# Attention groups scored one ahead and normalised one behind, with decay rows in bf16, rotation on one engine and a weight split at every side step

## The chip, the cores and the metric

One core of one Trainium2 chip runs the kernel. The metric is the device time of one execution in microseconds (us), lower is better. Engines are called PE (TensorE), DVE (VectorE), ACT (ScalarE), POOL (GpSimd) and SP (SyncE). The difference that a measurement of this kernel can tell from none is about 0.3%.

## What is computed

The reference runs two stacks of two layers on a sequence of 256 tokens with 1024 channels, in float32.

```
first_block, for layer 0 and 1:
    x = x + norm(mixer(norm(x)))       mixer: even_mixer (layer 0) or diff_mixer (layer 1)
    x = x + norm(memory_cross_attention(norm(x), norm(mem)))      4 heads of 64
    x = x + norm(swiglu(norm(x)))
even_mixer: fox attention, 8 heads: softmax(q k^T / 8 + (c_q - c_k)), c = cumsum(log_sigmoid(f)), causal
            nsa attention, 8 heads: compressed, selected and window keys, each gated by a sigmoid
diff_mixer: 8 heads: p = softmax(q1 k1^T / 8) - lam * softmax(q2 k2^T / 8), o = p v
second_block, for layer 0 and 1:
    x = x + 0.5 * swiglu_2(norm(x))
    z = norm(x) @ w_in; neighborhood attention (8 heads, a bias table), gated linear attention,
        latent attention (4 heads, 192 wide), each projected and gated; x = x + mixed @ w_out
    x = x + 0.5 * swiglu_2(norm(x))
partial rotation (rope) of q and k: x1' = x1 c - x2 s, x2' = x2 c + x1 s
```

A fox row's own term c_q cancels in the softmax, so the kernel adds only -c_k to the scores.

## The kernel before

**Weights.** All weight matrices are one stream of units of at most 2048 columns by 128 partitions. `load` (L419 on) brings a unit into one of 6 raw slots over SP's queue. `part` splits it: ACT casts it to fp32r (`w_hi`, L450), DVE subtracts that from the raw value (`w_lo`, L455), into 3 high slots. A product of two fp32 matrices is three fp32r matmuls (`three_products`, L594 to L596). Outside attention a unit is split in one piece, by `prepare`. Inside attention (`turn["gentle"]`) it is split in 4 pieces (PIECES), one at a time by `trickle`. When PE's next matmuls need a unit that isn't whole, `take` puts out all its missing pieces at once.

**Side work.** `fillers` is a list of generators (the input projections' later columns, memory keys and values, compression, gates). Each step of one, a side step, is some 12 matmuls on a quarter of a unit, or a group of transposes with its evictions. `fill(n)` puts out n side steps. Every engine runs its instructions in the order in which the Python puts them out, and waits on semaphores in that order.

**Attention** (`attention`, L777 on) takes groups of two heads: 16 groups in the even mixer (4 fox, then 4 times selected, window and compressed keys), 8 in the diff mixer, 2 in each memory attention, 4 in each neighborhood attention (with `bias`), 2 in each latent attention. A group's parts are:

- `scores`: PE writes two heads' scores into two banks. Mask rows come by bf16 matmuls (L806), q k^T by fp32 matmuls (L812); a fox group has a second fp32 matmul per score block with `ident` rows as weights and `c_neg` (8 partitions) as data.
- `maxed`: DVE takes the row maxima (L843) and scales them (L846); with a bias it first adds the bias (L836) and reduces that (L839).
- `exped`: ACT takes the exponentials into `probs` with their sums (L868).
- `normed`: DVE takes a reciprocal per head (L887), in gated groups a product with the gate (L890), and scales `probs` (L894).
- `turned`: PE transposes `probs` (L909), waiting for `normed`.
- `copied`: ACT (L922) and DVE (L928) copy the transposed weights into `pT`.
- `summed`: PE multiplies them with the values (L953 for the diff mixer, L959, L966). The result is evicted by ACT (L986) and DVE (L991, the low part), in the diff mixer by ACT alone (L977). In the even mixer the selected and window groups of a head pair are not evicted; their sum goes on in the compressed group.

The order of the parts is written out by hand at the end of `attention`:

```
for i in range(len(groups) + 1):
    trickle(2)
    scores(i); turned(i - 1); maxed(i)
    copied(i - 1); exped(i)
    fill(a); normed(i); summed(i - 1); fill(b)
```

The pair (a, b) is (3, 3) for the first groups of the two mixers and (1, 1) for the rest, (5, 5) in the neighborhood attention, (2, 2) in the latent one; memory attention has no side work. A group's `do` runs all side steps up to a named result (L1822 to L1823, L1943 to L1945).

**Rotation** (`rotate`, L1334) makes two products and one difference per token tile on DVE and two products and one sum on POOL (L1344, L1373, L1382); DVE's second part waits for POOL's products.

Of the kernel before, what the change touches and what calls it, by code (L numbers as in the profile page):

```python
# [16 lines left out]
P = 128  # L17
# [11 lines left out]
FOX_H = 8  # L29
NSA_H = 8  # L30
# [50 lines left out]
HI_SLOTS = 3  # L81
FF_CHUNK = 256
# [127 lines left out]
class Unit:  # L210
# [6 lines left out]
    def __init__(self, shape, parts, split=True):  # L217
        self.shape, self.parts, self.split = shape, parts, split
        self.used = self.landed = None
        self.whole = False  # L220

# [83 lines left out]
def program(nc, a, const_where, col_of, out):  # L305
    ctx = ExitStack()
    with ctx:
# [12 lines left out]
        def signal(name):  # L320
# [32 lines left out]
        probs = sb("probs", [P, 2, TT * T], over=("tmp", 0))  # L353
        pT = sb("pT", [P, 2, 2 * TT * P], over=("tmp", 2 * TT * T))
# [7 lines left out]
        up = sb("up", [GLA_RANK + 1, 2, T])  # L362
        posi = sb("posi", [P, TT], I32)
# [21 lines left out]
                "normed": pool_did.now(), "under way": iter(()), "gentle": False}  # L385
# [14 lines left out]
        def next_bank():  # L400
            while banks[turn["bank"] % 8].held:
                turn["bank"] += 1
# [63 lines left out]
        def free(of, n, slots):  # L466
            return n < len(of) and (n < slots or of[n - slots].used is not None)
# [38 lines left out]
        def to_T(nblk, src, dst, width=P, scale=None, group=2, dst_lo=None, ready=None, fills=0, after=None):  # L506
            groups = []
            fill(fills)
            for _ in to_T_steps(groups, nblk, src, dst, width, scale, group, dst_lo, ready, after):
# [3 lines left out]
        def to_T_steps(groups, nblk, src, dst, width=P, scale=None, group=2, dst_lo=None, ready=None, after=None):  # L513

            before = marks() if after is None else after
            for b0 in range(0, nblk, group):
# [20 lines left out]
                if turn["evac"] % 2 and dst_lo is None:  # L539
                    @block.vector  # L540
                    def _(dve):
# [5 lines left out]
                        if scale is None:  # L547
# [11 lines left out]
                def _(act):  # L559
# [5 lines left out]
                    if scale is None:  # L565
# [33 lines left out]
        def unit_steps(h, k0, u, nk, c, n, pair, there, evac, at=None):  # L599
# [4 lines left out]
            for tt in range(TT):  # L604
                ts_ = slice(tt * P, (tt + 1) * P)
                for ka in range(0, kk, step):
# [15 lines left out]
                    if last and tt == TT - 1:  # L622
                        u.used = pe_did.now()
                    if last and k0 + kk == nk:
# [152 lines left out]
        def attention(groups, after=None, plan=None):  # L777
# [39 lines left out]
            def maxed(i):  # L817
# [4 lines left out]
                for j in range(2):  # L822
                    @block.vector
                    def _(dve):
# [6 lines left out]
                        if g.get("bias"):  # L831
                            bias, there = g["bias"](j)
                            dve.wait_ge(*there)
                            if i > 0:
                                dve.wait_ge(*st[i - 1]["turned"][j])
# [1769 lines left out]
```

## Time and profile before

| | |
|---|---|
| median of 3 runs | 2435.87 us (2432.83 to 2440.7) |
| profiled execution, its own time | 2435.56 us |
| its span | 2433.9 us |
| PE busy | 2164.7 us, 89% of the span |
| DVE busy | 1266.0 us, 52% |
| ACT busy | 1024.7 us, 42% |
| POOL busy | 160.3 us, 7% |
| mean granted clock of PE | 0.927 |

The profiled execution's own time is within 0.02% of the median. A "busy" engine is one with an instruction under way. The granted clock is the share of PE's full clock (1.00 is 2.4 GHz, 0.50 is 1.2 GHz) that it had.

### The profile page before, as it was taken

The numbers are of one execution on the slowest core, as the hardware profiler recorded it, in microseconds if no ns is written. First come the engines' busy times: TensorE is split into PE (matmuls) and PEld (weight loads), VectorE is DVE, ScalarE is ACT, GpSimd is POOL, SyncE is SP. The second block draws the span as 40 slices with busy tenths as digits, with TensorE's granted clock in tenths as the row PEclk, the third lists the DMA queues.
The fourth block names the chain that finished last, engine by engine and source line by source line (L and its number), as shares of the span: only waits on it lengthen the run. The fifth ranks groups of instructions, "written<-read, shape, count | busy, mean of one in ns | idle before, by whom it ended". The sixth has DMA issues, their size and how long they took to land.

```text
span 2433.9 us, 26665 instructions
## 1 busy us (share of the span) xinstructions
PE 2164.7 (89%) x9943; PEld 1751.3 (72%) x9956; DVE 1266.0 (52%) x1767; ACT 1024.7 (42%) x1507; POOL 160.3 (7%) x200
## 2 busy tenths in 40 slices
PE   6968779989778999999879789999999978879998
PEld 5746658877567887887757657887887757757887
DVE  4335555555655555555546545555555545555554
ACT  4234444443444444344335344444444436334442
POOL 0010000000100000000301210000000302120000
PEclk8877879999889999999889979999999888979999
DMA  8212235554124554554523324655555534224553
GB/s 263 76 54 87 79 108 185 185 167 152 44 87 150 189 189 157 189 190 162 151 87 118 126 70 156 190 188 169 184 188 171 167 100 130 86 75 146 187 187 103
DMA packets 247751, 346.14 MB, mean 142 GB/s; under 512 B 28292, under 2 KB 177608, under 8 KB 247624
## 3 DMA queue, kind: packets, MB, share of 16 engines
q1 hardware_dynamic: 245816, 340.37, 43.6%
q10 hardware_dynamic: 1264, 2.79, 0.3%
q8 instruction: 81, 1.33, 0.2%
q0 software_dynamic: 544, 1.29, 0.2%
q14 instruction: 46, 0.38, 0.1%
HBM read 343.35 MB, written 2.33 MB: 142 GB/s over the span
## 4 chain that ended last, share of the span: by engine, by line
PE 76%; DVE 8%; issue 8%; ACT 4%; POOL 3%; ACTq 0%; DVEq 0%; POOLq 0%
PE bank L594 23%; PE bank L595 22%; PE bank L596 22%; DVE w_lo L455 3%; PE bank L812 1%; PE bank L959 1%; PE bank L1089 1%; PE bank L533 1%; ACT w_hi L450 1%; ACT h_hi L569 1%; DVE jobstat L843 1%; ACT probs L868 1%; DVE x L1250 1%; PE bank L953 1%; DVE h_lo L585 1%
## 5 line engine op out<-in xcount | busy, mean ns | idle before, releaser
L455 DVE TENSOR_TENSOR w_lo<-raw,w_hi 128x2048 fp32r<-128x2048 f32 (+5 forms) x453 | 735.5, 1644 | 501.0 <-ACT w_hi L450 500.2
L594 PE MATMUL bank<-w_hi,h_hi 128*128 128x512 f32 (+4 forms) x1936 | 786.1, 406 | 110.6 <-DVE w_lo L455 54.6
L595 PE MATMUL bank<-w_lo,h_hi 128*128 128x512 f32 (+4 forms) x1936 | 768.3, 397 | 0.0
L596 PE MATMUL bank<-w_hi,h_lo 128*128 128x512 f32 (+4 forms) x1936 | 766.9, 396 | 0.0
L450 ACT CAST w_hi<-raw 128x2048 fp32r<-128x2048 f32 (+5 forms) x453 | 613.6, 1380 | 292.9 <-PE bank L596 282.1
L594 PEld LDWEIGHTS bank<-w_hi,h_hi 128*128 128x128 f32 x1936 | 383.8, 198 | 201.7 <-issue 47.1
L596 PEld LDWEIGHTS bank<-w_hi,h_lo 128*128 128x128 f32 x1936 | 383.1, 198 | 75.3
L595 PEld LDWEIGHTS bank<-w_lo,h_hi 128*128 128x128 f32 x1936 | 384.7, 199 | 68.5
L594 PE MATMUL bank<-w_hi,ff_hi 128*128 128x512 f32 x528 | 206.0, 390 | 0.0
L596 PE MATMUL bank<-w_hi,ff_lo 128*128 128x512 f32 x528 | 205.5, 389 | 0.0
L595 PE MATMUL bank<-w_lo,ff_hi 128*128 128x512 f32 x528 | 205.5, 389 | 0.0
L1068 ACT ACTIVATE ff_silu<-bank,rs 128x256 f32<-128x256 f32 x132 | 55.6, 473 | 200.9 <-PE bank L596 200.9
L1100 ACT CAST ff_hi<-bank 128x512 fp32r<-128x512 f32 x66 | 38.7, 587 | 235.8 <-PE bank L1089 235.8
L594 PEld LDWEIGHTS bank<-w_hi,ff_hi 128*128 128x128 f32 x528 | 99.1, 188 | 21.1 <-DVE ff_lo L1105 0.7
L596 PEld LDWEIGHTS bank<-w_hi,ff_lo 128*128 128x128 f32 x528 | 99.1, 188 | 20.7
L595 PEld LDWEIGHTS bank<-w_lo,ff_hi 128*128 128x128 f32 x528 | 99.2, 188 | 20.2
L1105 DVE TENSOR_TENSOR ff_lo<-bank,ff_hi 128x512 fp32r<-128x512 f32 x66 | 45.6, 691 | 131.0 <-ACT ff_hi L1100 131.0
L1077 DVE SCALAR_TENSOR_TENSOR ff_hid<-bank,rs,ff_silu 128x256 f32<-128x256 f32 x132 | 57.8, 479 | 86.3 <-ACT ff_silu L1068 86.3
L699 POOL TENSOR_TENSOR rs<-rs,const 128x2 f32<-128x2 f32 (+2 forms) x27 | 32.0, 1184 | 1026.1 <-DVE rs L694 1026.1
L569 ACT ACTIVATE h_hi<-bank,cols 128x256 fp32r<-128x256 f32 x128 | 49.9, 482 | 79.1 <-PE bank L533 54.3
L812 PE MATMUL bank<-kT,qT 64*128 64x256 f32 (+2 forms) x320 | 68.1, 423 | 9.4 <-DVE kT L551 5.1
L585 DVE SCALAR_TENSOR_TENSOR h_lo<-bank,cols,h_hi 128x256 fp32r<-128x256 f32 x128 | 52.4, 476 | 41.7 <-ACT h_hi L569 41.7
(248 smaller groups left out, 1673.6 us busy)
## 6 DMA issues: line engine op xcount, KB each, us to landing
raw<-in_ffn_w SPq DMA_DIRECT2D x176, 512.0 KB, 4.5
raw<-in_w_in SPq DMA_DIRECT2D x52, 1024.0 KB, 5.1
raw<-in_ffn_w SPq DMA_DIRECT2D x44, 1024.0 KB, 4.9
raw<-in_ffn_wg SPq DMA_DIRECT2D x44, 512.0 KB, 4.0
raw<-in_ffn_wu SPq DMA_DIRECT2D x44, 512.0 KB, 5.0
raw<-in_ffn_wd SPq DMA_DIRECT2D x22, 1024.0 KB, 4.9
raw<-in_od_w_in SPq DMA_DIRECT2D x12, 1024.0 KB, 5.2
raw<-in_w_out SPq DMA_DIRECT2D x8, 1024.0 KB, 5.0
```

Source lines behind the costliest of these rows:

```text
L450: act.copy(hi[:, cs], raw_[:, cs]).then_inc(*act_did.up())
L455: dve.tensor_tensor(lo_[:, cs], raw_[:, cs], hi[:, cs].bitcast(F32), ALU.subtract).then_inc(*dve_did.up())
L569: act.activation(dst(b0 + b, 1), ps[:, b:b + 1, :], ACT.Copy, scale=scale(b0 + b)).then_inc(*act_did.up())
L585: dve.scalar_tensor_tensor(dst_lo(b0 + b, 1), ps[:, b:b + 1, :], scale(b0 + b), dst(b0 + b, 1).bitcast(F32), ALU.mult, ALU.subtract).then_ ...
L594: pe.matmul(out, x_hi, u.hi[:, k, cols_], start=start, stop=False)
L595: pe.matmul(out, x_hi, u.lo[:, k, cols_], start=False, stop=False)
L596: return pe.matmul(out, x_lo, u.hi[:, k, cols_], start=False, stop=stop)
L812: mm = pe.matmul(view(i, j)[:, tt, 0:g["n"][tt]], l, r, start=(m == 0 and not masked), stop=(m == len(pairs) - 1), skip_group_check=True)
L1068: act.activation(ff_silu[:, c % 2, tt, :], bank.t[:, 0:FF_CHUNK], ACT.Silu, scale=r(tt)).then_inc(*act_did.up())
L1077: dve.scalar_tensor_tensor(ff_hid[:, c % 2, tt, :], bank.t[:, FF_CHUNK:2 * FF_CHUNK], r(tt), ff_silu[:, c % 2, tt, :], ALU.mult, ALU.mult) ...
L1100: act.copy(ff_hi[:, c % 2, :, :], ps).then_inc(*act_did.up())
L1105: dve.tensor_tensor(ff_lo[:, c % 2, :, :], ps, ff_hi[:, c % 2, :, :].bitcast(F32), ALU.subtract).then_inc(*dve_did.up())
```

## The change

The order of the parts becomes this, with `begin(i)` for a group's `do` and `scores`:

```
begin(0)
for i in range(len(groups) + 1):
    trickle()
    maxed(i); exped(i)
    normed(i - 1); turned(i - 1)
    fill(a)
    copied(i - 1); begin(i + 1)
    fill(b)
    summed(i - 1)
```

`fill` puts out one split piece after each side step. The decay of a fox group is one bf16 matmul per head over both token tiles, with `c3` (72 partitions: three bf16 parts of -c) as data and `c_row` as weights. The factor 1/8 moves from the scores to the eviction of the transposed q (`times`), so the maxima need no scaling where the scale is 1. One reciprocal and at most one gate product serve both heads. `rotate` runs on DVE alone, both token tiles in one instruction. `probs` has two buffers, and `pT` moves to a gain buffer (in the neighborhood attention to `o_buf`). The diff, cut to its core:

```diff
+LAG = 1
 def fill(n=1):
             while n > 0 and fillers:
                 if next(fillers[0], None) is None:
                     fillers.pop(0)
-                else:
-                    n -= 1
+                    continue
+                n -= 1
+                turn["steps"] += 1
+                if turn["gentle"]:
+                    trickle()
 def free(of, n, slots):
-            return n < len(of) and (n < slots or of[n - slots].used is not None)
+            if n >= len(of) or n < slots:
+                return n < len(of)
+            late = turn["gentle"] and of is split_units
+            return of[n - slots].used is not None and not (late and turn["steps"] - of[n - slots].at < turn["lag"])
 def take():
             if turn["gentle"]:
                 load_more()
+                turn["lag"] = 0
                 while u.landed is None or (u.split and not u.whole):
                     trickle()
+                turn["lag"] = LAG
 scores:
+                for bank in s["banks"]:
+                    bank.held = True
+                    if g.get("decay"):
+                        for j in range(2):
+                            l, r = g["decay"](j)
+                            pe.matmul(view(i, j), l, r, start=False, stop=False, skip_group_check=True)
 maxed:
+                            plain = g["scale"] == 1.0 and not g.get("guard")
+                            if not plain:
+                                dve.wait_ge(*dve_did.now())
+                                dve.tensor_scalar(js[:, 4 + 2 * j:6 + 2 * j], peak, g["scale"], -NEG / 100, ALU.mult,
+                                                  ALU.min).then_inc(*dve_did.up())
 exped:
-                        if i > 0:
-                            act.wait_ge(*st[i - 1]["turned"][j])
+                        if i > 1:
+                            act.wait_ge(*st[i - 2]["turned"][j])
 normed:
+                    dve.wait_ge(*s["exped"][1])
+                    dve.reciprocal(recip, sums).then_inc(*dve_did.up())
...
                 for j in range(2):
-                        dve.wait_ge(*s["exped"][j])
-                        dve.reciprocal(r, sums).then_inc(*dve_did.up())
 rotate:
-                for tt in range(TT):
-                    products(dve, dve_did, tt, ((0, x1, cos), (1, x2, sin)))
-                    products(pool, pool_did, tt, ((2, x2, cos), (3, x1, sin)))
-                    dve.tensor_tensor(x1[:, tt], t[0][:, tt], t[1][:, tt], ALU.subtract).then_inc(*dve_did.up())
-                    pool.tensor_tensor(x2[:, tt], t[2][:, tt], t[3][:, tt], ALU.add).then_inc(*pool_did.up())
+                products(dve, dve_did, ((0, x1, cos), (1, x2, sin), (2, x2, cos), (3, x1, sin)))
+                dve.wait_ge(*dve_did.now())
+                dve.tensor_tensor(x1, t[0], t[1], ALU.subtract).then_inc(*dve_did.up())
+                dve.tensor_tensor(x2, t[2], t[3], ALU.add).then_inc(*dve_did.up())
 even mixer:
-                    return [(qT[b:b + HD, hp, tt * P:(tt + 1) * P], kT[b:b + HD, hp, 0:n]),
-                            (ident[0:FOX_H, 2 * hp + j:2 * hp + j + 1].broadcast_to([FOX_H, P]), c_neg[:, 0:n])]
+                def decay(j, hp=hp):
+                    return (c_row[:, 2 * hp + j:2 * hp + j + 1].broadcast_to([PARTS_C, P]),
+                            c3[:, :].unsqueeze(1).broadcast_to([PARTS_C, TT, T]))
```

## Rows read from the trace of the kernel before

**Rows 1.** The page: PE's granted clock in 40 slices, in tenths of full speed.
```profile
PEclk8877879999889999999889979999999888979999
```
**Rows 2.** Stretches of attention: start:end, length, busy time by engine, clock, DMA share, GB/s.
```profile
72.00:137.00 65.00, 57.90 (x230) 42.73 (x234) 21.75 (x57) 15.58 (x51) 0.00 (x0) 0.82 0.23 66
137.00:175.50 38.50, 22.48 (x103) 17.88 (x104) 14.09 (x42) 12.23 (x24) 7.23 (x30) 0.73 0.13 36
175.50:266.00 90.50, 72.42 (x434) 50.98 (x437) 58.59 (x206) 44.37 (x149) 0.00 (x0) 0.81 0.22 73
307.00:325.00 18.00, 10.52 (x53) 6.80 (x54) 10.63 (x28) 8.43 (x25) 0.00 (x0) 0.66 0.20 58
575.00:666.00 91.00, 71.54 (x380) 55.39 (x384) 52.13 (x142) 37.63 (x111) 6.48 (x13) 0.90 0.22 72
1184.00:1267.00 83.00, 65.25 (x288) 50.22 (x288) 38.61 (x77) 27.07 (x67) 5.92 (x8) 0.80 0.30 89
1416.00:1452.00 36.00, 35.67 (x128) 24.38 (x129) 12.19 (x31) 15.48 (x31) 0.00 (x0) 0.82 0.18 59
```
**Rows 3.** PE's waits (us in total, times, longest): whole span, then 137 to 175.5 us.
```profile
PE bank L594 <- DVE w_lo L455: 60.0, 13, 12.5
...
PE bank L909 <- DVE probs L894: 5.3, 3, 2.5
...
PE bank L594 <- DVE w_lo L455: 16.0, 2, 11.3
```
**Rows 4.** PE's waits in the diff mixer's attention, 575 to 666 us.
```profile
PE bank L953 <- DVE jobstat L887: 7.8, 4, 2.7
PE bank L594 <- DVE w_lo L455: 4.7, 2, 3.8
PE bank L594 <- DVE sq L1344: 4.2, 1, 4.2
```
**Rows 5.** PE's longest wait in sum, first neighborhood attention, 1184 to 1267 us.
```profile
PE bank L594 <- DVE w_lo L455: 8.5, 2, 6.2
```
**Rows 6.** Groups of instructions by form: shapes, count, busy us, mean ns of one, idle before.
```profile
L812 PE MATMUL bank<-hT,const 8*128 8x256 f32 x16 | 6.6, 496 | 0.0
L812 PE MATMUL bank<-hT,const 8*128 8x128 f32 x16 | 4.0, 334 | 0.0
L806 PE MATMUL bank<-bf_causal,bf_ident 128*128 128x512 bf16 x27 | 9.7, 402 | 4.5 <-DVE kT L548 2.0 <-ACT kT L566 1.0 <-issue 0.6
```
**Rows 7.** Timeline after a weighted sum, ACT and DVE, 1221 to 1226 us: start, us.
```profile
1221.26 0.37 ACT L986 CAST y_hi<-bank 128x256 fp32r<-128x256 f32 x1 [7.73 <-PE bank L959]
1221.53 2.18 ACT L450 CAST w_hi<-raw 128x512 fp32r<-128x512 f32 x4
1221.67 0.42 DVE L991 TENSOR_TENSOR y_lo<-bank,y_hi 128x256 fp32r<-128x256 f32 x1 [5.40 <-ACT y_hi L986]
1222.19 2.90 DVE L455 TENSOR_TENSOR w_lo<-raw,w_hi 128x512 fp32r<-128x512 f32 x4
```
**Rows 8.** DVE's maxima and norms by form, whole span.
```profile
L843 DVE TENSOR_REDUCE jobstat<-bank 128x2 f32<-128x512 f32 x56 | 38.4, 686 | 51.6 <-PE bank L812 51.6
L836 DVE SCALAR_TENSOR_TENSOR probs<-bank,gain 128x512 f32<-128x512 f32 x16 | 10.9, 683 | 0.9 <-PE bank L812 0.9
L846 DVE TENSOR_SCALAR jobstat<-jobstat 128x2 f32<-128x2 f32 x64 | 10.8, 169 | 2.2
L887 DVE RECIPROCAL jobstat<-jobstat 128x2 f32<-128x2 f32 x80 | 12.7, 159 | 5.7 <-ACT probs L868 4.8
```
**Rows 9.** DVE's scalings, timeline at 644 and 1214 us.
```profile
644.07 0.55 DVE L894 TENSOR_SCALAR probs<-probs,jobstat 128x128 f32<-128x128 f32 x2
...
1214.45 0.62 DVE L894 TENSOR_SCALAR probs<-probs,jobstat 128x256 f32<-128x256 f32 x2
```
**Rows 10.** Rotation in latent attention: the line's view, durations ns least/median/most.
```profile
L1344 DVE TENSOR_TENSOR sq<-z,const x8: 291/497/505, 1404.9 to 2149.8; 128x128 f32<-128x128 f32 x8
```
**Rows 11.** A stretch 4 us after PE's stall at 70 us, columns as in rows 2.
```profile
76.00:78.00 2.00, 2.00 (x5) 0.71 (x4) 0.00 (x0) 0.00 (x0) 0.00 (x0) 0.50 0.00 0
```

More of the change, by code:

```diff
@@ L384, in program @@
         turn = {"bank": 0, "evac": 0, "gain": 0, "taken": 0, "loaded": 0, "parted": 0,
-                "normed": pool_did.now(), "under way": iter(()), "gentle": False}
+                "normed": pool_did.now(), "under way": iter(()), "gentle": False, "steps": 0, "lag": LAG}
         block = ctx.enter_context(nc.Block())
@@ L400, in next_bank @@
         def next_bank():
+            assert not all(b.held for b in banks)
             while banks[turn["bank"] % 8].held:
@@ L775, in program, with flat, attention @@
         attended = {}
-        def attention(groups, after=None, plan=None):
+        def flat(v):
+            return v.rearrange("p (j w) -> p j w", j=2)
+        def attention(groups, pT, after=None, plan=None):
             before = after or marks()
@@ L994, in attention, with begin @@
             turn["gentle"] = True
-            for i in range(len(groups) + 1):
-                a, b = plan(i) if plan else (0, 0)
-                trickle(2)
+            def begin(i):
                 if i < len(groups):
@@ L1001, in attention @@
                     scores(i)
-                if i >= 1:
-                    turned(i - 1)
+            begin(0)
+            for i in range(len(groups) + 1):
+                a, b = plan(i) if plan else (0, 0)
+                trickle()
                 if i < len(groups):
@@ L1007, in attention @@
                         groups[i]["scored"]()
+                    exped(i)
+                if i >= 1:
+                    normed(i - 1)
+                    turned(i - 1)
+                    for bank in st[i - 1]["tbanks"]:
+                        bank.held = True
+                fill(a)
                 if i >= 1:
                     copied(i - 1)
-                if i < len(groups):
-                    exped(i)
-                fill(a)
-                if i < len(groups):
-                    normed(i)
+                begin(i + 1)
+                fill(b)
                 if i >= 1:
                     summed(i - 1)
-                fill(b)
             turn["gentle"] = False
@@ L1189, in load_gain, with spare_gain @@
             return gain[:, g, :], gain_landed[g].now(), g
+        def spare_gain(post_gain):
+            return gain[:, 1 - post_gain[2], :]
         class Sublayer:
@@ L1424, in _ @@
             def _(dve):
+                dve.memset(lf3[:, :, :, :], 0.0).then_inc(*dve_did.up())
+                dve.memset(c_row[:, :], 0.0).then_inc(*dve_did.up())
+                dve.wait_ge(*dve_did.now())
+                for m in range(3):
+                    rows_ = slice(32 * m, 32 * m + FOX_H)
+                    dve.tensor_copy(c_row[rows_, :], ident[rows_, rows_]).then_inc(*dve_did.up())
                 dve.wait_ge(*more_landed.now())
@@ L1571, in log_f, with _ @@
                 log_sigmoid((small[:, 80:96], small[:, 32:48], small[:, 48:64], small[:, 64:80]))
+                logged = dve_did.now()
+                @block.vector
+                def _(dve):
+                    dve.wait_ge(*logged)
+                    for m in range(3):
+                        dve.tensor_copy(lf3[:, :, m, 0:FOX_H], lfs).then_inc(*dve_did.up())
                 there["lf"] = marks()
@@ L1823, in even_mixer @@
             groups[FOX_G + 2]["do"] = lambda: until("short")
-            attention(groups, fox_turned, lambda i: (3, 3) if i < FOX_G else (1, 1))
+            attention(groups, flat(spare_gain(post_gain)), fox_turned, lambda i: (3, 3) if i < FOX_G else (1, 1))
+            gain_used[1 - post_gain[2]] = pe_did.now()
             while fillers:
@@ L1945, in diff_mixer @@
             groups[HH + 2]["do"] = lambda: written(0)
-            attention(groups, start, lambda i: (3, 3) if i < HH - 1 else (1, 1))
+            attention(groups, flat(spare_gain(post_gain)), start, lambda i: (3, 3) if i < HH - 1 else (1, 1))
+            gain_used[1 - post_gain[2]] = pe_did.now()
             written(1)
@@ L2135, in neighborhood @@
                                    out=(y_hi[:, hp, :], y_lo[:, hp, :])))
-            attention(groups, after, lambda i: (5, 5))
+            attention(groups, flat(o_buf[:, 0, :]), after, lambda i: (5, 5))
             y_there = attended["o"]
@@ L2544, in latent @@
                                         y_lo[:, 2 * hp:2 * hp + 2, :].rearrange("p h n -> p (h n)"))))
-            bias_free[:] = [rotated] * 4
-            attention(groups, None, lambda i: (2, 2))
+            attention(groups, flat(gain[:, 0, :]), None, lambda i: (2, 2))
+            bias_free[:] = [attended["o"]] * 4
             start_branch(2, attended["o"])
```

150 lines of the change are left out of this document (79 added, 71 removed).

## The prediction

> **What bounds the kernel now.** I read the page first. PE is busy for 89% of the span, and the row of its clock [rows 1] is at 9 in most slices and at 7 or 8 in some. Those slices are the attention stages and what lies around them; the feed-forward stages run PE without a gap at full clock, and the change doesn't touch them. Next the stretches of attention [rows 2]: the reader is to see length minus PE's busy time. Idle PE is 7.1 us in the fox groups (72 to 137 us), 16.0 while side work makes the sparse keys (137 to 175.5), 18.1 in the twelve sparse groups, 7.5 in a memory attention (there are two), 19.5 in the diff mixer, 17.8 in a neighborhood attention (two), 0.3 in a latent one (two). That is some 112 us, and the clock in these stages is 0.66 to 0.90. Last the waits of PE, to see what ends the idle time [rows 3 to 5]: the largest single item is a weight split that is late, 60.0 us in 13 waits, 16.0 of it at 137 to 175.5 us.
>
> **Decay.** The fox groups' decay takes 6.6 + 4.0 = 10.6 us of PE [rows 6] and becomes eight bf16 matmuls of 512 columns, the form of the mask. The mask's 27 recorded matmuls are busy 9.7 us, 0.36 each without their overlap: 8 x 0.3 = about 2.4 us. Gain 8.2 us, nearly all of it on the path, as PE is busy 57.9 of 65 us there [rows 2]. The five DVE instructions that build the bf16 parts, and the fills of zeros, are under 3 us in all by durations of 0.2 to 0.7 us for DVE operations [rows 8], and lie under the input projection; without that cover they would cost these 3 us.
>
> **Splits.** Before, only two pieces came per group, and a unit that was not whole was finished in one burst in front of PE's next matmuls. Now each side step brings its piece. I take all such waits inside attention as gone where the burst was the cause: 4.7 us in the diff mixer [rows 4], 8.5 in each neighborhood attention [rows 5], some 4 us in the fox groups, and 4.8 of the 16.0 us at 137 to 175.5 us [rows 3]; the rest of these 16.0 us is a chain through rotation, the gates' sigmoid and the memory's transposes, which stays. About 7 us more lies right behind attention, in the matmuls that found no split unit.
>
> **A stall that the new order brings.** This is the step that takes most back. In PE's queue `summed(i-1)` is now followed at once by `turned(i)`, with no side step and no scores between. `turned(i)` waits for `normed(i)`, which stands in DVE's queue behind the eviction of `summed(i-1)`, a split piece, and `maxed(i+1)`. DVE can't start on these until PE has ended the sum. So after each evicted sum PE waits for this chain [rows 7 to 9]: ACT's and DVE's eviction, 0.88 us from PE's end at 1221.21 us to 1222.09; one split piece, 0.73 + 0.1; two maxima, 2 x 0.69 + 0.05, or with a bias four instructions, 2.75; a reciprocal 0.20 with its wait, a gate product 0.2 where there is one; the first two scalings, 0.55 or 0.62. The sum is 0.88 + 0.83 + 1.43 + 0.2 + 0.55 + 0.1 = 4.0 us for a fox group, 5.4 us with a bias, and 4.1 us in the diff mixer, where ACT alone evicts but the split piece on ACT still waits behind that eviction. The last group has no maxima behind it: 2.5 to 2.9 us. If the split piece has nothing to do, 0.8 us less for these, and only 0.9 us in the diff mixer, since DVE then waits for nothing. Sparse groups that are not evicted: about 0.5 us. What is queued behind these waits on DVE is `maxed` and `normed` themselves, on ACT the exponentials, which have slack.
>
> The new idle time, stretch by stretch, in us: fox 2.0 (its start) + 2 x 4.0 = 10 (was 7.1). Sparse keys 16.0 - 4.8 - 1.2 (rotation) + 4.0 = 14. Sparse groups 4.0 + 3 x 3.9 + 8 x 0.5 + 1 (compression) = 20.7 (was 18.1). Memory 6.5 each (was 7.5). Diff mixer 1 + 4 x 4.1 + 2.5 + 1.7 + 2.1 (last copy) + 2 (rotation) = 25.7 (was 19.5). Neighborhood 2.5 + 0.5 + 2 x 5.4 + 1 + 2.5 + 1.1 = 18.4 each, against 17.8 and the 4.0 behind it. Latent 3.9 against 0.3 and 2.7 behind it.
>
> **Work saved on DVE.** Two scalings of maxima (0.17 each), one reciprocal (0.16) and often a gate product, with their waits, are some 0.8 us per group [rows 8]. In the fox and diff groups this lies on the stall above and is counted there. In the sparse groups DVE is busy 58.6 of 90.5 us [rows 2], so it isn't the bound, and I count nothing more.
>
> **Rotation.** A product of 128 columns on DVE takes 0.50 us in the middle and 0.29 at best, beside POOL [rows 10]. One instruction for both token tiles I price at 0.42 us, DVE's duration for 256 columns [rows 7]: six are 2.6 us where the pair of engines needs 3.1. That is 0.5 to 1.2 us per call, 2 us for the latent calls, besides what stands above. The Trainium skill (SBUF — State Buffer, Who interferes with whom) says that a DVE instruction with two SBUF inputs and a POOL one that reads SBUF exclude each other for their whole length; by that an old product would take 0.29 plus POOL's whole 0.46, 0.75 us, and the gain would be 1 us larger per call. The row has 0.50, and I go by it.
>
> **The sum.** Idle changes: +2.9 - 2 + 2.6 - 2 + 6.2 + 2 x (18.4 - 21.8) + 2 x (3.9 - 3.0) = +2.7; decay -8.2; rotation -2. This is -7.5. The clock: PE works at half for some us after a stall [rows 11], which show 0.50 at 76 us, after the stall at 70 us. PE's timeline has 36 gaps over 1.5 us in or right behind attention now, and about 33 are left by my list. At some 1 us lost for each, and with the split piece that is sometimes nothing (0.8 us less for five or so of the stalls), that is -7 at most, and I take -4. So 2435.56 - 11.5 = 2424 us. The profiled execution's 2435.56 stands 0.3 us under the median of 2435.87, so nothing is to be added.
>
> **Rivals.**
> 1. *Slower: the stall costs clock too.* The place is `turned(i)` behind `summed(i-1)`, the price 4.0 to 5.4 us idle, and it decides once each of the some 23 long stalls drags PE to half speed for about 8 us instead of the 4 us counted, 2 us of work lost more in 14 of them, 28 us in all: 2452 us. For it: after the stall of 2.0 us at 70 us the clock is still at that half 4 us later [rows 11]. Against it: the diff mixer has gaps of 2 to 4 us and keeps 0.90 [rows 2, 4]. The Trainium skill (TensorE: Matmul & The Clock Gate, HAM oscillation) warns of just this, matmuls in bursts between waits that start slow every time; by it the whole of each burst could be slow, and this case would be the rule.
> 2. *Faster by much: the stalls stay at their floor.* If the split piece mostly has nothing to do (side steps have made them all), the seven long stalls of the even mixer lose 0.8 each, the diff mixer's four 3.2 each, those of the neighborhood and latent stages 0.8: some 24 us with the rest. If PE then keeps the full clock it has at 0.80 to 0.83 now, a further 15 us return: 2385 us. Against it: a unit has four pieces and four side steps, so the extra `trickle` at the top mostly finds one.
> 3. *It cancels.* If bursts were not the cause of the late splits (the neighborhood's 6.2 us wait also has the bias in front), 8 to 10 us of the gain are missing: 2434 us.
> That the change would not do what it says isn't likely, as the order is explicit.
>
> **Numbers.** Forecast 0.45, rival 1 0.25, rival 2 0.17, rival 3 0.13. The measurement tells 0.3%, 7.3 us. Of the forecast's own range (2405 to 2436) four fifths are faster by more: 0.36, with rival 2 0.53. Within: 0.09 + 0.13 = 0.22. Slower: 0.25. The predicted time is the likeliest case's, 2424. The range takes in rival 2's centre and reaches to rival 1's: 2385 to 2450; the case's own range is 2405 to 2436.
>
> **What would show it.** Right: L812 with `hT` and `const` gone and PE's fox stretch shorter by 8 us; PE's waits for `w_lo` down from 60 to about 25 us; and PE's waits at the transposes (L909 before) for DVE's scalings up from 5.3 us [rows 3] to 60 or more, each 4 to 5 us, every one behind a weighted sum. The forecast is wrong if those waits at the transposes are under 2 us each (then rival 2), or if the clock in the attention stretches is under 0.75 (then rival 1).

## The result, and the profile after

The changed kernel takes 2498.45 us (median of 4 runs, 2491.01 to 2502.1), the kernel before 2437.33 us in the same measurement (4 runs, 2432.83 to 2440.7). The ratio is 1.0257, with a 95% interval of 1.0230 to 1.0284: slower by 2.6%. The forecast was 2424 us with a range of 2385 to 2450, so the result is outside it, on the other side of no change. It lies beyond rival 1 (2452) too.

The profiled execution took 2491.01 us, the shortest of the four, with a span of 2489.1 us and a mean granted clock of 0.915 (before: 0.927). These are the page's lines of PE, DVE and PE's clock, and its group of the transposes.

```profile
PE 2171.1 (87%) x9919; PEld 1759.7 (71%) x9932; DVE 1250.0 (50%) x1669; ACT 1024.4 (41%) x1501; POOL 134.7 (5%) x134
...
PEclk9876669999888999999879979999999888989999
...
L951 PE MATMUL bank<-const,probs 128*128 128x128 f32 (+1 forms) x264 | 60.7, 396 | 119.1 <-DVE probs L936 94.3
```

The span grew by 55.2 us. PE's idle time, span less busy, went from 2433.9 - 2164.7 = 269.2 us to 2489.1 - 2171.1 = 318.0, so 48.8 us of the growth are idle and 6.4 are busy, though the change takes matmuls away. The clock row has 6 where it had 8 and 7 in the slices of the even mixer [rows 1].

PE's waits over the whole span show what replaced the late splits of [rows 3] (us in total, times, longest; `issue` means that the profile shows nothing that PE waited for):

```profile
PE bank L951 <- DVE probs L936: 94.3, 29, 5.7
...
PE bank L951 <- ACT probs L901: 24.2, 6, 4.7
PE bank L613 <- issue: 16.5, 4, 6.2
PE bank L613 <- ACT w_hi L460: 11.6, 3, 8.7
PE bank L613 <- DVE w_lo L465: 10.7, 2, 9.4
```

The waits of these matmuls for split halves fell from 60.0 us for DVE's half and 10.6 for ACT's to 10.7 + 11.6 = 22.3. The waits at the transposes (L951, L909 before) rose from 5.3 us to 94.3 + 24.2 = 118.5 us in 35 waits. Five of these are under 0.7 us; the other 30, from 1.1 to 5.7 us, are called stalls here.

The stretches that answer to [rows 2] (start:end, length, busy time by engine, clock, DMA share, GB/s) are, in order: fox groups, sparse keys, sparse groups in two parts, memory attention, diff mixer, neighborhood, latent.

```profile
69.70:118.20 48.50, 36.29 (x181) 28.80 (x182) 21.43 (x46) 18.30 (x56) 0.00 (x0) 0.88 0.28 83
118.20:168.50 50.30, 27.09 (x119) 22.50 (x120) 15.62 (x43) 13.35 (x28) 2.83 (x12) 0.77 0.15 49
168.50:205.00 36.50, 28.35 (x144) 23.22 (x144) 10.91 (x30) 10.14 (x28) 0.00 (x0) 0.59 0.09 30
205.00:285.00 80.00, 58.69 (x295) 37.93 (x296) 37.90 (x129) 30.46 (x113) 0.00 (x0) 0.65 0.17 60
328.00:347.00 19.00, 10.72 (x55) 6.96 (x53) 6.84 (x17) 6.44 (x22) 0.00 (x0) 0.69 0.18 56
598.80:697.00 98.20, 73.10 (x377) 56.22 (x383) 52.14 (x127) 41.86 (x120) 1.64 (x1) 0.90 0.20 69
1214.00:1304.00 90.00, 66.08 (x295) 51.36 (x293) 43.96 (x84) 33.35 (x79) 5.88 (x8) 0.78 0.29 88
1450.00:1502.00 52.00, 41.99 (x139) 28.19 (x137) 17.61 (x37) 19.80 (x40) 0.00 (x0) 0.80 0.17 54
```

The sparse groups stand out: PE is busy for 87.0 of 116.5 us there and has a clock of 0.59 and 0.65, where the kernel before was busy for 72.4 us at 0.81 [rows 2]. One stall of the fox groups, in the timelines of PE, ACT and DVE (start, us, with the idle time before in brackets), shows the mechanism with every link:

```profile
96.95 0.60 PE L1003 MATMUL bank<-gain,z 128*64 128x256 f32 x6
...
97.60 0.37 ACT L1030 CAST oT_hi<-bank 128x256 fp32r<-128x256 f32 x1 [1.67 <-PE bank L1003]
97.87 0.56 ACT L460 CAST w_hi<-raw 128x436 fp32r<-128x436 f32 x1
...
98.00 0.42 DVE L1035 TENSOR_TENSOR oT_lo<-bank,oT_hi 128x256 fp32r<-128x256 f32 x1
98.46 0.61 DVE L465 TENSOR_TENSOR w_lo<-raw,w_hi 128x436 fp32r<-128x436 f32 x1
98.99 1.28 DVE L875 TENSOR_REDUCE jobstat<-bank 128x2 f32<-128x512 f32 x2
100.19 0.17 DVE L921 RECIPROCAL jobstat<-jobstat 128x4 f32<-128x4 f32 x1
100.58 1.01 DVE L936 TENSOR_SCALAR probs<-probs,jobstat 128x128 f32<-128x128 f32 x4 [0.23 <-DVE jobstat L921]
...
101.28 1.51 PE L951 MATMUL bank<-const,probs 128*128 128x128 f32 x6 [3.73 <-DVE probs L936]
```

The sum ends at 97.55, its eviction begins at 97.60, and everything from there to the scaling at 100.58 stands in one queue. The exponentials of the group that PE waits for had ended at 85.3; those of 99.71 on are the next group's. Behind the stall PE works at half speed for some 5 us; two of the windows there, the stretch right after the stall and one after it, have these rows:

```profile
101.30:105.00 3.70, 3.70 (x13) 3.52 (x14) 0.29 (x2) 0.13 (x2) 0.00 (x0) 0.50 0.00 0
106.00:113.00 7.00, 6.93 (x37) 5.55 (x37) 2.96 (x5) 3.07 (x6) 0.00 (x0) 0.97 0.04 9
```

### The profile page after: what moved, and what is told of

Its sections match the earlier page's. It is cut to its first block, busy times and chain, and to the rows that moved or that the text cites. A ratio compares the mean times of both kernels' runs of the same rounds, so it can differ in the third digit from the quotient of the medians.

```text
span 2489.1 us, 26399 instructions
## 1 busy us (share of the span) xinstructions
PE 2171.1 (87%) x9919; PEld 1759.7 (71%) x9932; DVE 1250.0 (50%) x1669; ACT 1024.4 (41%) x1501; POOL 134.7 (5%) x134
## 4 chain that ended last, share of the span: by engine, by line
PE 77%; issue 9%; DVE 7%; ACT 4%; POOL 1%; DMA 1%; DVEq 0%; ACTq 0%; SPq 0%; POOLq 0%
PE bank L613 23%; PE bank L614 22%; PE bank L615 22%; PE bank L951 2%; DVE w_lo L465 2%; PE bank L842 1%; PE bank L1137 1%; PE bank L1003 1%; ACT w_hi L460 1%; PE bank L548 1%; ACT h_hi L588 1%; ACT probs L901 1%; DMA raw<-in_ev_w_in 1%; DVE jobstat L875 1%; DVE x L1302 1%
## 5 line engine op out<-in xcount | busy, mean ns | idle before, releaser
L951 PE MATMUL bank<-const,probs 128*128 128x128 f32 (+1 forms) x264 | 60.7, 396 | 119.1 <-DVE probs L936 94.3
L951 PEld LDWEIGHTS bank<-const,probs 128*128 128x128 f32 (+1 forms) x264 | 45.2, 201 | 135.5 <-DVE probs L936 78.0
L615 PEld LDWEIGHTS bank<-w_hi,ff_lo 128*128 128x128 f32 x528 | 99.1, 188 | 20.7
```

Of the source, the lines that this page charges most:

```text
L615: return pe.matmul(out, x_lo, u.hi[:, k, cols_], start=False, stop=stop)
L951: m = pe.transpose(bank.t[0:kw, n * P:(n + 1) * P], probs[:, i % 2, j, tt * T + kb * P:tt * T + kb * P + kw], ident)
```

## The experiments

The results by stage help in reading what follows: us from a stage's first scores (or mask) to its last weighted sum, from PE's timeline, with PE's idle time in it in brackets where it was read. "Even" goes from the fox groups to the end of the first memory attention.

| kernel | even | diff | neighborhood 1 | latent 1 | median, us |
|---|---|---|---|---|---|
| before | 251.7 (54.1) | 91.1 (19.4) | 82.3 (17.0) | 35.0 (0.0) | 2435.87 |
| after | 277.2 (79.3) | 99.6 (24.1) | 86.8 (21.4) | 50.0 (8.3) | 2498.45 |
| e1_old_order | 239.2 (54.1) | 74.9 (9.2) | 65.6 (5.6) | 35.4 (0.0) | 2363.22 |
| e12_norm_in_place | 243.6 (60.0) | 82.4 (13.7) | 65.6 (6.1) | 40.2 (1.3) | 2381.28 |
| e2_norm_first | 260.9 (71.1) | 87.4 (15.8) | 78.3 | 47.4 | 2443.38 |
| e4_piece_late | 270.3 | 89.6 | 84.8 | 47.4 | 2466.20 |
| e6_pieces_only | 256.3 (56.6) | 77.8 (11.5) | 65.2 (5.3) | 34.9 (0.0) | 2391.17 |
| e7_decay_only | 234.2 | 92.1 | 82.3 | 35.0 | 2418.23 |
| e8_old_order_lag3 | 229.8 | 80.6 | 66.5 | 35.4 | 2359.14 |

The kernel before was measured again beside each batch: 2437.92, 2434.16 and 2438.00 us. Each ratio below is to the one of its batch.

### e1_old_order: all of the change but the order of the parts

```diff
-            begin(0)
-                trickle()
+                trickle(2)
+                begin(i)
+                if i >= 1:
+                    turned(i - 1)
                 if i < len(groups):
                     maxed(i)
...
+                if i >= 1:
+                    copied(i - 1)
+                if i < len(groups):
+                    exped(i)
+                fill(a)
+                if i < len(groups):
+                    normed(i)
                 if i >= 1:
                     summed(i - 1)
+                fill(b)
```

> The kernel after with only the hand-written order of the parts put back as it was (two split pieces at the top, scores, transposes, maxima, copies, exponentials, side steps, norm, sum, side steps); everything else of the change stays. Theory S (order): PE waits at the transposes for the scaled probabilities in the kernel after, 94.3 us in 29 waits with DVE's and 24.2 us in 6 with ACT's as the last to end, because nothing stands between a weighted sum and the next transposes. With the old order these go, the old tail waits come back, and the parts that should gain (decay, pieces per side step) are left: 2415 to 2440 us. Theory T (pieces): the split piece after every side step and the later use of slots are what delays DVE, whatever the order: 2475 us or more.

Measured: 2363.22 us, ratio 0.9690 (0.9662 to 0.9719), over 50 us below what theory S expected. The order alone is thus worth 2498.45 - 2363.22 = 135 us, and the rest of the change is 3.1% faster than the kernel before. On the page PE is busy for 2132.1 us of a span of 2363.9, so 231.8 us idle. Against after, idle is 86.2 us less and busy 39.0 us less in the two profiled executions, with the same matmuls in both. The 39 us are the clock: laid over the granted clock of each trace, PE's busy time at half clock is 311.2 us in after and 234.4 here, and half of that difference is 38.4 us. Of the waits at the transposes little is left; their rest and the two largest ones at the weighted sums are these:

```profile
PE bank L1003 <- ACT probs L901: 12.2, 5, 4.5
...
PE bank L951 <- DVE probs L936: 9.5, 7, 3.0
PE bank L1003 <- DVE gain L970: 8.6, 8, 2.3
```

### e12_norm_in_place: scores one ahead, but each group normalised in its own round

```diff
                 if i >= 1:
-                    normed(i - 1)
                     turned(i - 1)
                 fill(a)
                 if i >= 1:
                     copied(i - 1)
+                if i < len(groups):
+                    normed(i)
                 begin(i + 1)
```

> The kernel after with one half of its order taken back: a group's norm stands in its own turn again (behind the copies of the group before, ahead of the next scores), while the scores stay one group ahead; LAG 1. Theory S (the norm put one behind makes the stall): the transposes find their probabilities scaled, the 118 us of waits at the transposes fall under 30 us, and the time is 2365 us or less, like the old order. If it is the scores one ahead, or the sum with nothing behind it, that costs, the time stays over 2430 us.

Measured: 2381.28 us, ratio 0.9769 (0.9739 to 0.9799), some 16 us above what theory S expected. Putting one part ahead of the next scores, side steps, sum, split piece and maxima takes back 117 of the 135 us. In place of the 35 waits at the transposes, three are left for the scalings, and in the fox groups the transposes follow the sum without a gap. This is PE's wait in the whole span, and then the timeline of PE at one of the fox groups' sums:

```profile
PE bank L951 <- DVE probs L936: 6.5, 3, 3.0
...
104.57 0.87 PE L1003 MATMUL bank<-gain,z 128*64 128x256 f32 x8
105.37 0.87 PE L951 MATMUL bank<-const,probs 128*128 128x128 f32 x6
```

The six transposes take 0.87 us here and 1.51 us behind the stall. The windows of the even stage and of the first neighborhood attention show both costs, first for e12:

```profile
72.30:315.80 243.50, 183.50 (x962) 139.26 (x962) 109.68 (x288) 91.83 (x269) 4.22 (x14) 0.78 0.23 72
1164.80:1230.40 65.60, 59.48 (x288) 46.77 (x288) 40.65 (x78) 31.04 (x74) 7.04 (x8) 0.84 0.36 113
```

and then for the changed kernel:

```profile
69.70:346.90 277.20, 197.89 (x954) 150.17 (x960) 110.03 (x288) 92.55 (x269) 4.23 (x14) 0.73 0.20 64
1217.20:1304.10 86.90, 65.46 (x288) 50.91 (x288) 40.76 (x78) 31.27 (x74) 5.88 (x8) 0.77 0.29 85
```

The neighborhood attention has 288 matmuls, 288 weight loads, 78 DVE and 74 ACT instructions in both, and takes 65.6 or 86.9 us. Here the place of `normed` is the only difference, so this is shown, not argued. The remaining 18 us between e12 and e1 come with the rest of the new order, the scores that are one ahead above all: 246.4 us idle (2379.4 - 2133.0) against 231.8, mostly in the even stage (5.9 us), the diff mixer (4.5) and the latent ones (1.3 each). That rest of the order gave nothing here, even without the stall.

### e2_norm_first: the norm of the last group ahead of the split piece and the next maxima

```diff
             for i in range(len(groups) + 1):
                 a, b = plan(i) if plan else (0, 0)
+                if i >= 1:
+                    normed(i - 1)
+                    turned(i - 1)
                 trickle()
                 if i < len(groups):
                     maxed(i)
                     exped(i)
-                if i >= 1:
-                    normed(i - 1)
-                    turned(i - 1)
```

> The kernel after with the norm and the transposes of the group before put ahead of the split piece, the maxima and the exponentials of the group itself. Theory S: the stall loses the maxima (1.5 us, with a bias 2.8) and the split piece (0.8), and keeps eviction and norm, some 1.7 us: about 35 stalls become 2.4 us or more shorter, so 2400 to 2425 us, and the waits for the scaled probabilities fall from 118 to 40 us or less. Theory T: no change beyond 10 us.

Measured: 2443.38 us, ratio 1.0020 (1.0005 to 1.0035), so 55 us come back, less than the 73 to 98 that theory S expected. The wait is shorter but not gone, as DVE still starts on the norm only after the sum and its eviction:

```profile
PE bank L951 <- DVE probs L936: 63.8, 28, 3.0
```

Its longest wait is 3.0 us instead of 5.7. In the first fox groups the three are 2.76, 1.88 and 1.98 us, where the changed kernel has 4.48, 3.73 and 3.87.

### e4_piece_late: only the split piece at the top moved behind the transposes

```diff
-                trickle()
                 if i < len(groups):
                     maxed(i)
                     exped(i)
                 if i >= 1:
                     normed(i - 1)
                     turned(i - 1)
+                trickle()
```

> The kernel after with the one split piece at the top of a group moved behind the transposes, nothing else. Theory S: a stall is shorter by 0.8 us where the piece stood in it, and in the diff mixer, where the piece ties DVE to ACT's eviction, by up to 3 us: 2455 to 2475 us. If the piece is mostly empty, 2490 us and above.

Measured: 2466.20 us, ratio 1.0116 (1.0084 to 1.0148), as expected. The piece's share of the order's cost is 32 us, in some 30 stalls: a little over 1 us each, for 0.7 us of ACT's and DVE's time in the chain and the clock behind it.

### e3_sum_early and e5_sum_early_lag3: side work between the sum and the transposes

```diff
                 begin(i + 1)
-                fill(b)
                 if i >= 1:
                     summed(i - 1)
+                fill(b)
```

> The kernel after with the weighted sum put ahead of the second batch of side steps, so that these steps stand between the sum and the next transposes. Theory S: in the groups with side work DVE has these steps' time for eviction, piece, maxima and norm; the stalls of 4 us (fox, first half of the diff mixer) and 5.6 us (neighborhood) fall under 1.5 us, those without side work and the first one of a stage stay: 2430 to 2455 us. Theory T: no change beyond 10 us.

Measured: 2522.15 us, ratio 1.0344 (1.0313 to 1.0376). That is 24 us more than the changed kernel, which neither theory had. The waits at the transposes are 107.0 us in 31 and 24.6 us in 5. The trace of a fox stall shows a split piece whose high slot PE has only just released: ACT's casts at 113.48 waited for PE, and DVE's differences, maxima, reciprocal and scalings follow one by one.

```profile
113.48 1.14 ACT L460 CAST w_hi<-raw 128x512 fp32r<-128x512 f32 x2 [2.40 <-PE bank L615]
...
114.13 1.29 DVE L465 TENSOR_TENSOR w_lo<-raw,w_hi 128x512 fp32r<-128x512 f32 x2 [2.25 <-ACT w_hi L460]
```

PE's transposes begin at 117.63, after 4.25 us. e5 is the same kernel with `LAG = 3`, so that a slot counts as free three side steps after its last use, not one.

> The kernel with the sum ahead of the second side steps, and a split piece allowed only when the unit that holds its slot was used three side steps ago instead of one (LAG 3). Theory P (pieces tie DVE to PE): in e3_sum_early ACT's split piece at 113.48 us waits for PE to end the last side step, whose matmuls are the last use of the piece's slot, and DVE's piece, maxima and norm wait behind it; so the stall stays though the sum's eviction is out of it. With LAG 3 the slot is long free, DVE has its work done during the side steps, and the stalls of the fox, diff and neighborhood stages fall under 1.5 us: 2380 to 2430 us. Theory E (it is the evictions alone): the change of LAG does nothing, 2500 us or more.

Measured: 2501.88 us, ratio 1.0265 (1.0237 to 1.0293), which is far from what theory P expected. The fox stall shown above falls from 4.25 to 1.95 us, so there the slot was the link. The two fox stalls before it stay at 4.48 and 3.96 us, so there it wasn't. In the neighborhood attention the stall stays at 6.28 us, for another reason, which the timelines of ACT, DVE and PE show:

```profile
1274.52 0.69 ACT L702 ACTIVATE z<-bank,rs 128x512 f32<-128x512 f32 x1 [4.26 <-PE bank L615]
1275.10 1.13 ACT L460 CAST w_hi<-raw 128x512 fp32r<-128x512 f32 x2
...
1275.74 1.29 DVE L465 TENSOR_TENSOR w_lo<-raw,w_hi 128x512 fp32r<-128x512 f32 x2 [1.99 <-ACT w_hi L460]
1276.96 0.69 DVE L866 SCALAR_TENSOR_TENSOR probs<-bank,gain 128x512 f32<-128x512 f32 x1
...
1280.76 1.94 PE L951 MATMUL bank<-const,probs 128*128 128x128 f32 x8 [6.28 <-DVE probs L936]
```

The last side step's own output (`z`, L702) is evicted by ACT at 1274.52, right after PE's last matmul. ACT's split pieces wait behind it, DVE's behind these, and the maxima and the norm behind them. A side step is no cover when its tail enters the queues that PE will wait for.

### e6_pieces_only, e7_decay_only and e11_rotation_only: three parts of the change, each added alone to the kernel before

e6 has the piece per side step and the rule for slots, with the old order and its `trickle(2)`:

```diff
+                n -= 1
+                turn["steps"] += 1
+                if turn["gentle"]:
+                    trickle()
```

> The kernel before with one part of the change: a split piece after each side step, and the rule for slots with LAG 1; its order of parts and its two pieces at the top stay. The old order with the rest of the change took 2363 us, 74 us under the kernel before. Theory P1: most of it is from the pieces (bursts gone in the neighborhood stages, which no other part touches and which fell from 82 to 65 us): 2385 to 2400 us. Theory P2: it is from decay, rotation and the fewer DVE instructions: 2425 us or more.

Measured: 2391.17 us, ratio 0.9816 (0.9793 to 0.9839), 43 us faster, as theory P1 expected. In the first neighborhood attention PE's idle time is 5.3 us, where it was 17.0, and in the diff mixer 11.5, where it was 19.4. The even stage gained nothing from it: 256.3 us, idle 56.6. The reason is in its sparse keys, where the three waits told below for the changed kernel are 8.83, 8.47 and 7.90 us here.

e7 has the bf16 decay (`c3`, `c_row`, `lf3` and their DVE instructions) in the scores of the fox groups:

```diff
+                    if g.get("decay"):
+                        for j in range(2):
+                            l, r = g["decay"](j)
+                            pe.matmul(view(i, j), l, r, start=False, stop=False, skip_group_check=True)
```

> The kernel before with only the decay as three bf16 parts (scaled by 8, as the scores here are scaled later). By my term: 8.2 us of PE less in the fox groups and nothing else, 2427 to 2431 us. If the clock gains too, 2422 us.

Measured: 2418.23 us, ratio 0.9934 (0.9908 to 0.9960), 16 us faster, more than expected. PE's four groups of fox scores, mask to last matmul, take 6.9 us in its timeline and took 20.4. The window of the fox groups has a clock of 0.96, where it was 0.82 [rows 2]. The second row is e6, which keeps the old decay, has no stall in the fox groups, and has a clock of 0.90:

```profile
72.00:119.00 47.00, 39.77 (x215) 31.57 (x219) 22.52 (x60) 16.00 (x52) 0.00 (x0) 0.96 0.30 91
...
68.80:122.20 53.40, 53.20 (x237) 39.37 (x239) 26.59 (x66) 20.09 (x59) 0.00 (x0) 0.90 0.27 80
```

e11 has the rotation on DVE alone:

```diff
-                for tt in range(TT):
-                    products(dve, dve_did, tt, ((0, x1, cos), (1, x2, sin)))
+                products(dve, dve_did, ((0, x1, cos), (1, x2, sin), (2, x2, cos), (3, x1, sin)))
```

> The kernel before with only the rotation on DVE, both token tiles in one instruction. By my term 2 to 5 us less: 2429 to 2433 us. If DVE's longer work holds up the splits behind it, 2436 us or more.

Measured: 2435.56 us over 12 runs, ratio 0.9986 (0.9969 to 1.0002): no difference that can be told from none.

### e10_order_alone: the change without the pieces

```diff
-                if turn["gentle"]:
-                    trickle()
...
-            late = turn["gentle"] and of is split_units
+            late = False
...
-                trickle()
+                trickle(2)
```

> The kernel after with the pieces part undone: no split piece after a side step, the rule for slots as before, two pieces at the top. The order cost 135 us with the pieces in (2498 against 2363). Theory S says that it costs about as much without them, as the stall is made of evictions, pieces at the top, maxima and norm: kernel before less decay and the small parts, some 2405 us, plus 110 to 140: 2515 to 2545 us. If order and pieces cost only together (theory P), 2450 us or less.

Measured: 2563.46 us, ratio 1.0514 (1.0485 to 1.0542), some 18 us over what theory S expected. So the order costs as much without the pieces. This is after with two pieces at the top of a round, both in the chain between the sum and the transposes, and with late splits besides:

```profile
PE bank L949 <- DVE probs L934: 121.0, 31, 6.3
PE bank L611 <- DVE w_lo L463: 40.3, 10, 13.1
PE bank L949 <- ACT probs L899: 37.3, 8, 4.7
```

### e8_old_order_lag3 and e9_turned_first: the way past both kernels

e8 is e1 with one line changed, `LAG = 3` for `LAG = 1`.

> The kernel of e1_old_order (old order, rest of the change) with LAG 3 instead of 1. In that order the norm ends long before the transposes, so theory P has little to gain: 2355 to 2368 us. If pieces that wait for PE also hold up DVE's maxima and copies there, 2345 us or less.

Measured: 2359.14 us, ratio 0.9685 (0.9662 to 0.9707), clock 0.941, as expected. It is the fastest kernel of this study, 3.15% under the kernel before. From e1, with 2363.22 us (2359.44 to 2365.56) in another batch, it can hardly be told. e9 is e8 with `turned(i - 1)` ahead of the scores and `copied(i - 1)` ahead of `maxed(i)`.

> The kernel of e8_old_order_lag3 (2359 us) with two swaps: the transposes of the group before ahead of the scores, and its copies ahead of the maxima. Where a stage has no side work left, the weighted sum there waits for a copy that stands behind maxima or exponentials (8.6 us and 12.2 us of waits in e1_old_order). If that is what is left, these waits halve: 2345 to 2355 us. If the transposes then wait for the norm instead, 2359 us or more.

Measured: 2382.74 us, ratio 0.9776 (0.9750 to 0.9801), 24 us slower than e8 in spite of a part that starts earlier. Without the scores between the sum and the transposes, DVE's scalings are awaited again:

```profile
PE bank L951 <- DVE probs L936: 42.9, 18, 3.9
```

So the scores of the old order were not idle filling. They are PE's work while DVE finishes the norm. Which share the second swap, the copies, has in the 24 us was not measured.

## Why the prediction was wrong

**The stall behind the sum: right place, right size where I looked.** I had 4.0 us for a fox group, 4.1 in the diff mixer, 5.4 with a bias. Behind an evicted sum the trace has 3.73 and 3.87, then 4.06, 4.05 and 4.05, and 5.59 twice. The waits for `w_lo` fell to 10.7 us (I had about 25), with 11.6 for `w_hi` beside them.

**The step that failed is "the new idle time, stretch by stretch".** The sum had +2.7 us for all idle changes; they were +48.8. Of the miss of 46.1 us, three terms of that list have 37.8: the sparse keys and groups 18.0, the two neighborhood attentions 11.0 (23.9 us idle in each window, where I had 18.4), the two latent ones 8.8. The rest is small: 3.6 in the memory attentions, 2.2 in the fox groups.

- *Sparse keys, 14 us, and sparse groups, 20.7 us, together 34.7.* Measured: 50.3 - 27.1 = 23.2 us, and in the two windows of the sparse groups 8.2 + 21.3 = 29.5 us, together 52.7. The stalls of the sparse groups are not the miss. There are seven, 22.1 us in sum: five stand behind an evicted sum (3.1 to 4.7 us), as I had it, and two behind a sum that isn't evicted (1.70 and 1.09 us, where I had 0.5). The miss is in the sparse keys. I took 4.8 of the 16.0 us of late splits there as gone, and the idle time became 6.2 + 8.7 + 7.5 = 22.4 us. The ten kernels with a piece per side step all have the last two of these waits (8.3 to 8.7 and 7.2 to 8.0 us); before, e7, e10 and e11, without it, do not. The timelines of ACT and PE show why:

```profile
147.22 0.62 ACT L460 CAST w_hi<-raw 128x512 fp32r<-128x512 f32 x1 [14.00 <-DMA raw<-in_ca_wv]
147.74 0.83 ACT L588 ACTIVATE h_hi<-bank,cols 128x256 fp32r<-128x256 f32 x2
...
163.60 1.14 ACT L460 CAST w_hi<-raw 128x512 fp32r<-128x512 f32 x2 [4.69 <-DMA raw<-in_ca_wv]
...
168.47 0.63 PE L832 MATMUL bank<-bf_causal,bf_ident 128*128 128x512 bf16 x1 [7.52 <-DVE hT L1739]
```

Twice a split piece of the memory's weights stands first in ACT's queue and waits for its load, which SP put out at 141.8 and 158.6 us and which landed at 147.2 and 163.6. What PE needs next (`h_hi` with `h_lo`, then `qT`, `kT` and `hT`) stands behind it, though it needs none of these weights. In the kernel before, `h_hi` was evicted ahead of the pieces, and PE waited 4.68 us at that place. A piece at every side step thus has a cost of its own, in either order of the parts, where its load has not landed.
- *Neighborhood, "2.5 + 0.5 + 2 x 5.4 + ...".* I gave the first transposes of this stage 0.5 us. They have no sum in front of them and still waited 5.71 us, behind the eviction of the last side step (DVE L687), two pieces and the maxima with their bias. The first transposes of the fox groups (4.48 us) and of the diff mixer (4.40) wait as long, where my list has 2.0 and 1 us for the start of the stage. My sign that every such wait would stand behind a weighted sum was wrong for these. The timelines of PE and DVE have it:

```profile
1239.86 0.75 DVE L687 TENSOR_SCALAR z<-bank,rs 128x512 f32<-128x512 f32 x1 [0.72 <-PE bank L615]
1240.53 1.28 DVE L465 TENSOR_TENSOR w_lo<-raw,w_hi 128x512 fp32r<-128x512 f32 x2
1241.73 0.68 DVE L866 SCALAR_TENSOR_TENSOR probs<-bank,gain 128x512 f32<-128x512 f32 x1
...
1245.53 1.94 PE L951 MATMUL bank<-const,probs 128*128 128x128 f32 x8 [5.71 <-DVE probs L936]
```

- *Latent, 3.9 us.* Measured 8.3 in each of the two: 5.23 us before the first transposes, for the same reason, and 3.03 before the second.

**The clock, -4 us.** Together with the decay's -8.2 I expected PE to be busy for 12 us less. It was busy for 6.4 us more, a miss of 18.6. Laid over the granted clock, PE's busy time at half clock rose from 276.1 us before to 311.2 after. Half of that, 17.6 us, is time lost to the clock, 14.0 of it in the even stage (78.7 to 106.8 us at half clock); everything else fell by 11.1 us. So the term's sign was wrong, and what failed is its price by count. I set 33 gaps over 1.5 us against 36 old ones, at 1 us each. Over the whole span there are 68 against 65, and the cost is 17.6 us. Against e1 it is 39.0 us for 30 stalls, 1.3 us each.

Rival 1 named the clock, with 8 us at half speed behind a stall. In the fox groups and the diff mixer this lasts 3 to 6 us. In the sparse groups the clock is at half for 37 us twice, from 178.1 and from 253.2, with some full clock between. The second stretch has three stalls, and e1 is at half for 10 us there. The first is not the stalls' alone: PE works there through 64 matmuls with 45 columns (the compression), and e1 has the same matmuls with no gap between them at the same clock:

```profile
168.90:182.40 13.50, 13.50 (x64) 13.45 (x64) 1.21 (x3) 1.71 (x4) 0.00 (x0) 0.50 0.22 78
```

The mark that I had set for rival 1, under 0.75, was met in the sparse groups, and besides only in the memory attention (0.69, where it was 0.66). The Trainium skill (TensorE: Matmul & The Clock Gate, HAM oscillation) describes bursts between waits that each start slow. The trace agrees in part: within 1 us of the end of each of the first three fox stalls the clock is at 0.50, but the diff mixer kept 0.90 in spite of four stalls of 4 us.

The misses add up: 46.1 us of idle time, 18.6 us of busy time and the 2.0 that I had set apart for the rotation are the 66.7 us by which the span passes my 2433.9 - 11.5 = 2422.4.

**Why I thought the order nearly free.** The prediction weighed a new order with pieces against the old order without them, and let the stalls of the one cancel against the late splits of the other. e6 and e1 show that they have little to do with each other: the old order with pieces has lost most late splits and has no such stalls. Idle fell by 269.2 - 231.8 = 37.4 us from before to e1, and the bursts that I had listed (4.7 + 2 x 8.5 + 4 + 4.8 + 7) are 37.5 us. That the two agree is luck, as the parts do not: the even stage gained none of it, and the diff mixer and each neighborhood attention some 10 to 12 us. The order was worth nothing in return, and cost 135 us.

**The other terms.** *Decay, -8.2 us:* e7 measured -16. I took the busy time of the removed matmuls' rows [rows 6], 10.6 us, for their price. In PE's timeline the fox scores fell by 20.4 - 6.9 = 13.5 us, so that price was too low. The rest goes with the clock of the stretch, 0.82 before and 0.96 in e7. *Rotation, -2 us:* -2.4 by the medians, no difference that can be told. *Work saved on DVE, 0:* pieces, decay and rotation alone add up to -43 - 16 - 2.4 = -61 us, and e1 has -75. The 13 us between them belong to what was never run alone (the folded 1/8, one reciprocal for two heads, the second buffer of `probs`) or to parts acting together. This stays open.

**What stays open** besides: whether `LAG = 3` helps e12 as it did one fox stall of e3; whether the sparse keys' waits go when a piece is put out only once its load has landed; and whether any part of "scores one ahead" would pay if a group's maxima and its norm both had their side work in front of PE. None of these was tried.

## What to carry to other kernels

When parts of a pipeline are moved, ask for every wait of the engine that bounds the kernel: what stands in the other engine's queue ahead of the awaited instruction, and which of it can't start before the waiting engine's own last instruction has ended. Anything that can't (an eviction, a copy, a split piece whose slot has just come free or whose load has not landed) is idle time in full, and "one behind" makes it worse, since it puts a norm that was long ready to run behind a later round's work. Price each part of a change against the best version without it, not against the kernel before, or a gain of one part will hide the loss of another.

## What the runs showed of the hardware

- The clock has a cost that stands in busy time: with equal matmuls, 30 stalls made PE 39.0 us busier (2171.1 against 2132.1 us). The 264 transposes alone took 60.7 us, against 41.5 + 2.9 in the kernel before.
- A busy PE can keep the half clock. In e1, 64 matmuls with 45 columns ran for 13.5 us without a gap at 0.50; the kernel before has 0.50 in the same matmuls. Why is not shown.
- Without 32 matmuls that have 8 rows of weights, the fox groups' clock was 0.96 instead of 0.82 (e7). That these few rows hold the clock down is not shown: e6 keeps them, has no stall among them, and has 0.90.
- A product of the rotation that has 256 columns takes DVE 0.42 us. Two of 128 columns beside POOL took 0.50 each [rows 10], and the first of each call, which starts just ahead of POOL's, 0.29. The Trainium skill (SBUF — State Buffer, Who interferes with whom) has the two engines exclude each other for a whole instruction. By that POOL's 0.46 us would have come on top, and the row has less, so full exclusion is not what it shows; taking POOL's share away changed the time by 0.14%, within what the measurement can tell.
